# Attention taken two pieces at a time on one turn bank, with the RWKV gate moved into it, in a three-block kernel on one core

## What is computed

```
p = rms_norm(h) @ w_in
p_tm = p[:SHIFT_COLS] + (prev - p[:SHIFT_COLS]) * mu_shift
r, k, v, w_lo, a_lo = split(p_tm)
w = -softplus(-(w0 + tanh(w_lo) @ w_up)) - 0.5 ; a = sigmoid(a0 + a_lo @ a_up)
y_rwkv = (group_norm(recurrence(r, w, k, v, kk, a)) * ln_w + ln_b + bonus) * silu(gate)
for window, dilation in ((128, 1), (512, 4), (2048, 16)):
    s = q k^T / 8 over the band, masked; m = max(s); l = sum(exp(s - m))
    o = exp(s - m) v / l ; lse = m + log(l)
y_att = sum_d softmax_d(lse) o_d * silu(att_gate)
h = h + concat(y_rwkv, y_att) @ w_out
```

## Time and profile before

| | us |
|---|---|
| median of 3 runs (lowest, highest) | 3029.09 (3027.73, 3030.66) |
| the profiled execution | 3025.99 |
| its span, first to last instruction | 3024.7 |
| PE busy | 2816.0 (93%) |
| DVE busy | 1654.0 (55%) |
| ACT busy | 1261.6 (42%) |
| POOL busy | 361.0 (12%) |

### The profile page before, as it was taken

The page is one execution under the profiler, slowest core; times in us unless marked ns, Lnnn a source line. Parts: engine busy times, 40 slices in busy tenths (PEclk is TensorE's granted clock), DMA queues, the critical chain, the costliest instruction groups (busy, mean ns, idle before and its releaser), DMA issues. The chain is left out here.

```text
span 3024.7 us, 52664 instructions
## 1 busy us (share of the span) xinstructions
PE 2816.0 (93%) x21272; PEld 2197.5 (73%) x21272; DVE 1654.0 (55%) x3101; ACT 1261.6 (42%) x2314; POOL 361.0 (12%) x525
## 2 busy tenths in 40 slices
PE   8999999999998999999999999996878899999998
PEld 6767777776666777677777777775777777778776
DVE  3555665753466435655555465574566664652565
ACT  4343534332134445555563443442444334532234
POOL 0000000000000011111110047764440000000000
PEclk9999999999999999999999999998998999999999
DMA  3011111224234532233332335347433464421114
GB/s 117 28 42 36 36 56 35 64 64 171 79 105 139 170 112 72 72 80 86 79 93 66 123 124 169 127 141 284 144 114 138 142 217 132 153 80 45 35 63 153
DMA packets 188369, 316.58 MB, mean 105 GB/s; under 512 B 78288, under 2 KB 119520, under 8 KB 186464
## 3 DMA queue, kind: packets, MB, share of 16 engines
q1 hardware_dynamic: 188128, 313.23, 32.7%
HBM read 239.19 MB, written 73.99 MB: 104 GB/s over the span
## 5 line engine op out<-in xcount | busy, mean ns | idle before, releaser
L259 PE MATMUL ps<-xs,wparts 128*128 128x512 f32 (+1 forms) x1664 | 699.3, 420 | 11.8 <-DVE xs L1528 9.3
L261 PE MATMUL ps<-xs,wparts 128*128 128x512 f32 (+1 forms) x1664 | 654.8, 394 | 0.0
L260 PE MATMUL ps<-xs,wparts 128*128 128x512 f32 (+1 forms) x1664 | 654.1, 393 | 0.0
L327 DVE TENSOR_TENSOR wparts<-wring,wparts 128x1024 fp32r<-128x1024 f32 x248 | 305.7, 1233 | 318.7 <-ACT wparts L319 295.2
L259 PEld LDWEIGHTS ps<-xs,wparts 128*128 128x128 f32 (+1 forms) x1664 | 313.5, 188 | 134.7 <-issue 72.1
L319 ACT ACTIVATE wparts<-wring 128x1024 fp32r<-128x1024 f32 x248 | 263.3, 1062 | 283.2 <-PE ps L261 220.0
L261 PEld LDWEIGHTS ps<-xs,wparts 128*128 128x128 f32 (+1 forms) x1664 | 312.7, 188 | 71.8
L260 PEld LDWEIGHTS ps<-xs,wparts 128*128 128x128 f32 (+1 forms) x1664 | 314.1, 189 | 58.6 <-issue 3.9
L2284 POOL COPY perm<-qkg 128x1024 f32<-128x1024 f32 x32 | 63.1, 2009 | 1488.7 <-ACT qkg L363 1092.0
L2430 ACT ACTIVATE Pm<-Pm,ml 128x128 f32<-128x128 f32 (+1 forms) x384 | 168.5, 442 | 140.9 <-DVE ml L2498 140.9
L2498 DVE CUSTOM_DVE_ANT_0 Pm<-ps,mask 128x128 f32<-128x128 f32 (+1 forms) x384 | 110.9, 348 | 187.9 <-PE ps L2333 187.9
(11 more groups left out here) (411 smaller groups left out, 4856.3 us busy)
## 6 DMA issues: line engine op xcount, KB each, us to landing
wring<-in_wo SPq DMA_DIRECT2D x96, 512.0 KB, 3.5
ops<-rw SPq DMA_DIRECT2D x32, 640.0 KB, 6.0
wring<-in_w SPq DMA_DIRECT2D x39, 512.0 KB, 3.5
wring<-in_w2u SPq DMA_DIRECT2D x33, 512.0 KB, 4.4
wring<-in_wg SPq DMA_DIRECT2D x24, 512.0 KB, 3.5
wring<-in_w2v SPq DMA_DIRECT2D x24, 512.0 KB, 4.1
wring<-in_w2a SPq DMA_DIRECT2D x24, 512.0 KB, 6.6
MB<-wst SPq DMA_DIRECT2D x48, 256.0 KB, 5.0
```

The source lines that it names most:

```text
L259: nc.tensor.matmul(out, a, c, start=start, stop=False)
L260: nc.tensor.matmul(out, b, c, start=False, stop=False)
L261: return nc.tensor.matmul(out, a, d, start=False, stop=stop)
L327: K.nc.vector.tensor_tensor(W.part(i, 1), W.raw(i), W.part(i, 0).bitcast(F32), ALU.subtract).then_inc(*K.dve.done("w_lo", W.first + i))
```

## The change

- A piece pair, called a duo, is the unit of attention: five duos a pass, seven rounds each. Round 0 has the values of duo g - 2 and the scores of duo g, one behind the other; rounds 1 to 4 have one turn each of duo g - 1 (one piece, one head: three or four blocks); rounds 5 and 6 have none. Duos are counted through all pairs, so that the last duos of a pair are finished in the first rounds of the next pass; after the eighth come two duos more without new scores.
- PSUM: scores four banks, turns one, outputs one (one output group, the second of dilation 16, takes the turn bank). DVE makes the minimum of one side (a piece, a head), then the copy of the side before; ACT makes the exp of one side per round.
- The RWKV gate is a fourth unit of each pass of attention: 32 steps, paced 11 in 12. It is brought out with Silu to a buffer of its own and stored by SP (`rg_store`). The last pass holds three units, paced 2 in 3.
- The preparation has three units a pair; four of them (three of the first pair, one of the second) run behind the attention. Its passes hold 3, 3, 3, 3, 3, 2, 2, 1 units. The last triangles start 17 rounds into the last pass.
- POOL solves two pairs at a time on 128 partitions. SP's order in attention and preparation changes with this: values for dilation 16 and the gate's store now stand ahead of the weights' way through memory, and in the last pass the first RWKV unit's load stands behind it. wup and reset64 are loaded during the end of attention.

```diff
-OUT_W0, V_W0, ATT_W0, PREP_W0, LATE_W0 = 47, 71, 95, 119, 152
+OUT_W0, V_W0, ATT_W0, PREP_W0, LATE_W0 = 47, 71, 95, 127, 152
...
-            + [A["w2a"][i] for i in range(24)] + [A["w2u"][i] for i in range(33)])
+            + [A["w2a"][i] for i in range(32)] + [A["w2u"][i] for i in range(25)])
...
+BEHIND, PASSES, LAST_AT = [(0, 0), (0, 1), (0, 2), (1, 0)], [3] * 5 + [2, 2, 1], 17
...
+    order = iter([(p, x) for p in range(NP) for x in range(3)][len(BEHIND):])
+    return [[next(order) for _ in range(n)] for n in PASSES]
...
 def prep_sp(K, A, B):
     nc, sp = K.nc, K.sp
-    nc.sync.dma_start(B.reset64, A["c2c"][:, 320:1344]).then_inc(*sp.done("reset", by=16))
-    nc.sync.dma_start(B.wup, A["wup2"]).then_inc(*sp.done("wup", by=16))
     nc.sync.dma_start(B.mar[:, :], A["c2c"][:, 0:128]).then_inc(*sp.done("mar", by=16))
+    first = [1 + len(BEHIND) + sum(PASSES[:p]) for p in range(NP)]
+    i = 6
     for p in range(NP):
-        for i in range(4 * p + 3 if p else 6, 4 * p + 7):
-            if i < 33:
+        for at in (first[p] + 3, first[p] + 4, first[p] + 5):
+            while i <= min(at, 24):
                 yield from w_load(K, B.W, i)
-            if i in MB_AT:
-                yield from mb_store(K, A, B, MB_AT.index(i))
-            if i in SOLVE_AT:
-                yield from solve_move(K, A, B, SOLVE_AT.index(i))
-        if p:
-            yield from prep_store(K, A, B, p - 1)
-    yield from mb_store(K, A, B, NP - 2)
+                i += 1
+            if at == first[p] + 3 and p:
+                yield from mb_store(K, A, B, p - 1)
+            if at == first[p] + 4 and p in (2, 4, 6):
+                yield from solve_move(K, A, B, p // 2 - 1)
+        if p < NP - 1:
+            yield from prep_store(K, A, B, p)
...
 def prep_early_sp(K, A, B):
-    for i in (1, 2):
+    for i in range(3):
         yield from w_load(K, B.W, i)
     K.sp.wait_ge(*(yield "a_s", 6, LAST[0]))
     K.sp.wait_ge(*(yield "perm", 6, 2))
     K.nc.sync.dma_start(B.cols[:, 0:96], A["c2"]).then_inc(*K.sp.done("c2", by=16))
+def prep_scans_sp(K, A, B):
+    sp = K.sp
+    sp.wait_ge(*(yield "a_s", 7, LAST[0]))
+    sp.wait_ge(*(yield "perm", 7, 2))
+    K.nc.sync.dma_start(B.wup, A["wup2"]).then_inc(*sp.done("wup", by=16))
+    sp.wait_ge(*(yield "att_out", 6))
+    K.nc.sync.dma_start(B.reset64, A["c2c"][:, 320:1344]).then_inc(*sp.done("reset", by=16))
...
-            at = 5120 if name == "bonus" else 6144
-            nc.sync.dma_start(A["rw"][p][:, at:at + 1024], src).then_inc(*sp.done("rw_store", p, name, slot=b, by=16))
...
+    G = B.G[:, :].rearrange("p (i t) -> p i t", t=32)
...
+    for u in BEHIND:
+        yield from prep_unit_pe(K, B, *u)
...
+    B.RM = at.RT.join(at.RO, at.RS.part([2, 3]))
     for p, units in enumerate(prep_groups()):
-        yield from weave(in_turn(*[prep_unit_pe(K, B, *u) for u in units],
-                                 *([triangles_pe(K, B, p), rwkv_first_pe(K, B.rw, B.RU)] if p == NP - 1 else [])),
-                         prep_small_pe(K, B, p), *([triangles_pe(K, B, p - 1)] if p else []))
+        yield from weave(in_turn(*[prep_unit_pe(K, B, *u) for u in units]),
+                         *([later(LAST_AT, in_turn(triangles_pe(K, B, p), rwkv_first_pe(K, B.rw, B.RU)))]
+                           if p == NP - 1 else []), prep_small_pe(K, B, p), *([triangles_pe(K, B, p - 1)] if p else []))
...
+        return x + (4 * p - 2 if p else 0)
...
+    return 4 * p + x + (2 if p < 7 else 0)
...
+ND2 = NS // 2
+def duo(g):
+    return divmod(g, ND2) if 0 <= g < 8 * ND2 else None
+def side(g, j):
+    (p, d), (x, h) = duo(g), divmod(j, 2)
+    return p, 2 * d + x, h
+def shelf(B, g, j):
+    return B.Pm[:, (4 * g + j) % 6, :]
+def duos(p):
+    return range(ND2 * p, ND2 * p + (ND2 if p < 8 else 2))
...
-        for i in range(3 * p + 4, 3 * p + 7):
+        for i in range(4 * p + 4, 4 * p + 8):
             if p < 7:
                 yield from w_load(K, B.W, i)
-            if p and i == 3 * p + 4:
+            if p and i == 4 * p + 4:
+                yield from values_load(K, A, B, p, 2)
+                yield from rg_store(K, A, B, p - 1)
                 yield from weights_move(K, A, B, p - 1)
         if p == 7:
             yield from prep_early_sp(K, A, B.prep)
...
         if p:
             yield from att_store(K, A, B, p - 1)
         yield from stats_move(K, A, B, p)
-        for pi in (1, 2):
-            if p < 7:
-                yield from values_load(K, A, B, p + 1, pi)
+        if p < 7:
+            yield from values_load(K, A, B, p + 1, 1)
     yield from w_load(K, B.prep.W, 3)
+    yield from prep_scans_sp(K, A, B.prep)
     yield from weights_move(K, A, B, 7)
     for i in (4, 5):
         yield from w_load(K, B.prep.W, i)
+    yield from rg_store(K, A, B, 7)
     yield from att_store(K, A, B, 7)
+    sp.wait_ge(*(yield "rg_store", 7))
     sp.wait_ge(*(yield "att_store", 6))
     sp.wait_ge(*(yield "att_store", 7))
...
+def rg_store(K, A, B, p):
+    K.sp.wait_ge(*(yield "uev", ATT_W0 + att_unit(p, 3), 1))
...
+def values_pe(K, B, p, n):
+    nc, pe, s = K.nc, K.pe, PIECES[n]
+    if s.first:
+        ring = B.RT if (s.pi, s.gg) == (2, 1) else B.RO
+        _, old = ring.take(("a_o", p, s.pi, s.gg), ("a_osc", p, s.pi, s.gg))
+        if old:
+            pe.wait_ge(*(yield old))
...
+def turn_pe(K, B, g, j):
+    nc, pe, (p, n, h) = K.nc, K.pe, side(g, j)
+    bank, old = B.RT.take(("a_t", p, n, h), ("a_pt", p, n, h))
+    pe.wait_ge(*(yield "a_exp", p, n, h))
+    if old:
+        pe.wait_ge(*(yield old))
+    for x, b in enumerate(PIECES[n].blocks):
+        a = nc.tensor.transpose(bank[:, half(x, 128)], shelf(B, g, j)[:, b[0]:b[0] + 128], K.ident)
+    a.then_inc(*pe.done("a_t", p, n, h))
...
+    for g in duos(p):
+        for x in range(2):
+            if duo(g - 2):
+                yield from values_pe(K, B, *side(g - 2, 2 * x)[:2])
+        for x in range(2):
+            if duo(g):
+                yield from scores_pe(K, B, *side(g, 2 * x)[:2])
+        yield STEP
+        for j in range(4):
+            if duo(g - 1):
+                yield from turn_pe(K, B, g - 1, j)
+            yield STEP
+        for _ in range(2):
+            yield STEP
...
-                         units(K, B, p + 1) if p < 7 else paced(fill(K, B), 1, 2))
-    yield from weave(tail(K, B, 7), behind(K, B.prep, 0))
+                         paced(units(K, B, p + 1), 11, 12) if p < 7 else paced(fill(K, B), 2, 3))
+    yield from weave(main(K, B, 8), tail(K, B, 7), behind(K, B.prep, 0))
...
-    B.RS, B.RT, B.RO = rows.part([0, 1]), rows.part([2, 3]), rows.part([4, 5])
+    B.RS, B.RT, B.RO = rows.part([0, 1, 2, 3]), rows.part([4]), rows.part([5])
...
+    if x == 3:
+        old, dst = [("rg_store", p - 1)] if p else [], B.rg
...
+    for g in duos(p):
+        for j in range(5):
+            if j < 4 and duo(g):
+                yield from max_dve(K, B, g, j)
+            if j and duo(g - 1):
+                yield from turn_dve(K, B, g - 1, j - 1)
+            yield STEP
+        for _ in range(2):
+            yield STEP
...
-    yield from solve_move(K, A, B.prep, NP - 2)
+    yield from solve_move(K, A, B.prep, NP // 2 - 1)
...
-    for p in range(8): L+=[c(0,p),c(1024,p),c(2048,p),c(G0,p)]
+    for p in range(8): L+=[c(0,p),c(1024,p),c(2048,p)]
...
+    A["w2a"]=units([c(A0,0),c(A0+1024,0)]+[x for p in range(7) for x in (c(A0,p+1),c(A0+1024,p+1),c(AG,p),c(G0,p))]+[c(AG,7),c(G0,7)])
```

More of the change, by code:

```diff
@@ L2104, in prep_pool @@
     nc.gpsimd.memset(B.mbs[:, :, 128:192], 0.0).then_inc(*pool.done("mb_zero"))
[L2105 to L2106 removed]
+    for j in range(NP // 2):
+        yield from solve_pool(K, B, j)
 def att_layout(K, A, st, xs, W, b1):
@@ new lines, in scores_pe @@
+def scores_pe(K, B, p, i):
+    nc, pe, s = K.nc, K.pe, PIECES[i]
+    qk = [B.qkg[:, p % 2, x, :] if s.pi == 0 else B.perm[:, s.pi - 1, x, :] for x in range(2)]
+    banks = [B.RS.take(("a_s", p, i, h), ("a_max", p, i, h)) for h in range(2)]
+    if s.pi == 0:
+        pe.wait_ge(*(yield "uev", ATT_W0 + att_unit(p, 1), 1))
+    else:
+        pe.wait_ge(*(yield "perm", p, s.pi))
+    for _, old in banks:
+        if old:
+            pe.wait_ge(*(yield old))
+    for c, two, lo, hi in s.cells:
+        for rr, (bank, _) in zip(RH, banks):
+            a = nc.tensor.matmul(bank[:, lo:hi], qk[0][rr, half(c, 128)],
+                                 qk[1][rr, 128 * (c - 1) if two else 128 * c:128 * c + 128], start=True, stop=True)
+    a.then_inc(*pe.done("a_s", p, i))
@@ new lines, in values_pe @@
+def values_pe(K, B, p, n):
[5 more added lines that the diff above has]
+            pe.wait_ge(*(yield old))
+    ob = K.bank["a_o", p, s.pi, s.gg]
+    pe.wait_ge(*(yield "a_pt", p, n, 1))
+    pe.wait_ge(*(yield "vc", p, s.pi))
+    for x, (lo, c, kc, new, end) in enumerate(s.blocks):
+        for h, rr in enumerate(RH):
+            a = nc.tensor.matmul(ob[rr, half(c % 4, 128)], B.Vc[:, 8 * s.pi + kc, rr], B.PT[:, n % 2, h, half(x, 128)],
```

(48 more changed lines are left out.)

266 lines of the change are left out of this document (86 added, 180 removed).

## The result

The changed kernel takes 3053.58 us (median of four runs, 3049.81 to 3063.51) where the kernel before, run beside it, takes 3029.88. The ratio is 1.0084, with an interval of 1.0063 to 1.0105: slower by 0.8%. The prediction was 3008.0 with a range of 2982 to 3033, and faster.

What follows compares the result with a forecast made beforehand. TensorE's own instructions were taken to bound both stages, save in drains and at the preparation's two ends. Attention +59.8 and preparation -81.2 gave -21.4 us: 3004.6 profiled, 3007.7 as median, so 3008, range 2982 to 3033.

Steps and rivals of the forecast that it cites:

- TensorE's own prices: Steady attention pass: 32 unit steps at 1.37 us, 43.7, plus values, scores, turns and seams, 26.5; together 70.2 us.
- rival 4: Preparation: three-unit passes held by VectorE or mask stores give back half a unit each, 22 us, 3030; chance 0.09.
- Rival 1: Attention: cheaper seams, no 3.2 us of waits a pass, no last-pass hole; 20 us less, 2988; chance 0.17.
- the price of a collision: Attention: 1024-column product or split, 1.40 us with GpSimd working, makes TensorE wait; three places a pass, 1.1 us.
- open round: Attention: three rounds a pass lack a unit step; two stand at a turn, about 1 us wait each, 2.1 together.
- The clock: Last attention pass: 1.7 us added for the clock, which fell after a similar hole.
- Rival 2: Attention: next piece's row minimum delays the single bank's copy, 0.35 us on 160 turns, +56, 3064; chance 0.11.
- Rival 3: Attention: third unit's split comes 3.5 us too late for VectorE in seven passes, +24, 3032; chance 0.10.
- The load in the last pass: Last attention pass: first RWKV unit's load stands behind the weights' way; TensorE waits about 6.4 us.
- Rival 5: Attention: ScalarE holds the projections' banks, TensorE waits some 2 us a pass, +16, 3024; chance 0.05.
- First preparation pass: One unit less, -10.9 us, and 3.6 of holes given back: 58.06 to 43.5, or -14.6.
- Last preparation pass: One unit, bound by the chain's latency: 32 us for 42.30, -10.3; bounds 28 and 40.

Runs made afterwards that it cites:

- the two earlier loads: Against the changed kernel, weight loads of preparation units 0 and 6 issued ahead of the weights' way and the barrier respectively: 3038.13 us, ratio 1.0042.
- both placements: Against the changed kernel, VectorE's additions at rounds 20 and 26, rounds without a unit step at 13, 27, 34, plus the two earlier loads: 2996.36 us, ratio 0.9892.

## Why the prediction was wrong

It failed by its own mark, a pass over 76. The kernel became slower where it was to become faster. Against its terms:

| part | forecast | measured | off by |
|---|---|---|---|
| first attention pass | 67.9 | 68.9 | +1.0 |
| six steady passes | 438.6 | 469.4 | +30.8 |
| last attention pass | 74 | 77.4 | +3.4 |
| behind | 49.9 | 51.5 | +1.6 |
| first preparation pass | 43.5 | 49.9 | +6.4 |
| four of three units | 177.1 | 177.2 | +0.1 |
| two of two units | 77.8 | 79.1 | +1.3 |
| last | 32 | 39.0 | +7.0 |
| end | 26 | 23.5 | -2.5 |

The 30.8 of the steady passes are 6 x 2.7 of waits, 5 x 1.7 of clock and 6 x 1.0 of work.

- **TensorE's own prices held.** Work of 70.9 us in a steady pass against 69.9; 72.07 with two banks, which by my prices is 69.9 and 2 for scores taken apart. The preparation at 44.3 a pass held four times, so rival 4 is out. Rival 1 is out with waits of 5.9 us a pass. Slips in the sum are small: 25.00 us over 110 are 0.2273 and not 0.2277, the scores come to 8.5 and the turns to 6.1; together they move a pass by about 0.1 us.
- **The step that failed is the price of a collision.** I took 1.40 us for a product with GpSimd at work, and 1.1 us a pass for three such places. It was 2.62 and 3.03 us, and it fell on a turn of an open round, which I had named as the rounds that can't hide a copy and priced at 1 us each with VectorE free. Both terms were there, and I added them as if they never met. The product of the earlier trace rows began when the GpSimd operation beside it had 0.31 us to go; the additions of O met copies that had 1.5 and 1.9 us to go. And the addition took up to 2.19 us in the trace of before already. Both are rows of before, by source line and from GpSimd's timeline:

```profile
L2552 DVE TENSOR_TENSOR O<-O x16: 1224/1472/2186, 1207.3 to 1656.8; 128x1024 f32<-128x1024 f32 x16
```

```profile
2022.45 1.35 POOL L1787 TENSOR_TENSOR solve<-solve,step 64x150 f32<-64x150 f32 x1
```

- **What the step explains.** Without the collision (GpSimd's copies later) the kernel takes 3025.5: 28 us of the 46 by which the forecast of 3007.7 was too low. That kernel is not faster than before either. The other 18 lie mostly in the two ends of the preparation and the last attention pass, below.
- **The clock.** I priced it only for the last pass. Behind the waits of 2.74 to 2.77 us, windows of 3.4 us show 0.50 to 0.55 in five of the six passes, 1.7 us each, and 1.00 in the first. This row too was at hand: in the last pass of before a wait of 2.94 us was followed by 0.50 (there, a wait of 2.42 was followed by 1.00).

```profile
1593.15:1596.55 3.40, 3.22 (x15) 2.53 (x16) 3.37 (x5) 1.80 (x7) 0.00 (x0) 0.50 0.00 0
```

- **Rival 2 was close and yet not it.** It put the row minima ahead of the copy on all 160 turns, 0.35 us each. 25 waits hold 38.0 us instead, and with both placements one bank is as quick as two. Its sum, 3064, was nearer to the result than the forecast by luck, since its mechanism is another.
- **Rival 3** did not occur in the steady passes: TensorE waited for no split there. The load in the last pass did what I said, with a hole of 8.84 where I had 6.4: 2.4 of the 3.4 us by which that pass is off. **Rival 5** is out: ACT's 47 us of 78 hold no bank.
- **First preparation pass.** I gave back 3.6 us of its holes for the earlier constants and named the loads behind the barrier as next. They were next, and cost more than the constants had: a wait of 7.06 us and two windows of 3.4 us at 0.50 and 0.55 behind it, where before had a wait of 2.3 and one such window. The pass is 2.7 us longer than the old one less a unit (47.1).
- **Last preparation pass.** I added up the chain's own instructions, 32 us. VectorE worked 26.07 us, and stood 5.4 for ScalarE and 5.8 for stores ahead of two mask products, for which the 32 have 4 with the products themselves; where the stores were out of the way, TensorE's order stood behind them. What one chain's instructions add up to leaves out what stands ahead of them on their engines.

What stays open: the waits of 1.4 and 2.2 us late in the last attention pass, at open turns, were not tried apart (behind the 2.2 the clock fell to 0.68 and 0.81 in two windows of 3.4 us), nor were the 1.6 us by which the units behind it came out longer and the 2.5 by which the end came out shorter. How long the last preparation pass would be without GpSimd beside it was not tried either.

## What to carry to other kernels

When an order is packed tighter, list for every engine's longest instruction what runs beside it now and what will run beside it then, and price it by its longest row, not by another instruction's. An estimate from above is its own time and the whole of the other's: 1.22 and 1.99 here, 3.2 us, where 3.03 was the longest measured. A round that hides nothing, a ring of one bank and a stretched instruction cost 0.7 to 1.4 us of wait at that turn with one of them moved and some 4 us more a pass where they meet; it is enough to move one of the three. Where two waits stand ahead of the same instruction, taking one away shows nothing, so try both together before either is given up.

## What was not expected of the hardware

- Between VectorE and GpSimd the loss is not a share of speed but a wait for the other's whole instruction: an addition of 1.22 us became 2.62 and 3.03, and a reordering copy of 2.0 became 3.0. VectorE's copies out of PSUM stayed at 0.55 to 0.56.
- A single wait of 2.74 to 2.77 us ahead of TensorE was followed by 3.4 us at about half the clock at the same place in five of six passes, and in six of six with the two earlier loads (0.50 to 0.59). A wait of 2.22 us was followed by 0.68 here, by 0.53 with the earlier loads and by 1.00 with GpSimd's copies later. Waits of 1.3 to 1.7 were followed by none. So the length of the wait alone does not decide it between 2.2 and 2.8 us; what does is not shown.
